# Two layers of a hybrid encoder on one core: part of the feed-forward down projections by seven products

## The reference, cut to what matters

```
def rmsnorm(x, g):
    xf = xf * lax.rsqrt(jnp.mean(xf * xf, axis=-1, keepdims=True) + EPS)
    return (xf * g).astype(x.dtype)

def swiglu(h, w_gate, w_up, w_down):              # 1024 -> 2816 -> 1024
    return (jax.nn.silu(h @ w_gate) * (h @ w_up)) @ w_down

x += 0.5*SwiGLU(RMSNorm x); x += Mixer(RMSNorm x); x += 0.5*SwiGLU(RMSNorm x)
```

## Time and profile before

| | |
|---|---|
| profiled execution, its own time | 1818.21 us |
| its span | 1816.3 us |
| TensorE busy | 1797.4 us (99%) |
| VectorE busy | 1331.8 us (73%) |
| ScalarE busy | 857.8 us (47%) |
| GpSimd busy | 51.7 us (3%) |
| DMA queue of SyncE | 174.49 MB, 31.4% of 16 engines |

### The profile page before, as it was taken

How to read it: one execution, slowest core, us unless ns; L and a number is a source line. 1 busy time by engine, 2 the same in 40 slices (tenths; PEclk the granted TensorE clock), 3 DMA queues, 4 the chain that set the end, 5 groups by cost and what they waited for, 6 DMA issues and landing times.

```text
span 1816.3 us, 32636 instructions
## 1 busy us (share of the span) xinstructions
PE 1797.4 (99%) x13408; PEld 1716.0 (94%) x13408; DVE 1331.8 (73%) x1826; ACT 857.8 (47%) x1403; POOL 51.7 (3%) x68
## 2 busy tenths in 40 slices
PE   9999999999999999999999999999999999999997
PEld 8999999999999999999999999999998899889986
DVE  7766887556768866887798578865646799578854
ACT  7443554335446543554565335543423565335542
POOL 0000000000000000000000000000123000000000
PEclk9999999999999999999999999999999999999999
DMA  5255233342222233223223332334222222332331
GB/s 179 84 96 117 94 117 102 108 126 69 60 81 81 94 100 102 97 99 110 89 93 101 102 101 93 108 103 123 84 70 70 70 84 103 109 101 94 111 113 56
DMA packets 81107, 176.87 MB, mean 97 GB/s; under 512 B 7292, under 2 KB 12700, under 8 KB 80960
## 3 DMA queue, kind: packets, MB, share of 16 engines
q1 hardware_dynamic: 80544, 174.49, 31.4%
q10 hardware_dynamic: 416, 0.29, 0.0%
HBM read 171.35 MB, written 3.41 MB: 96 GB/s over the span
## 4 chain that ended last, share of the span: by engine, by line
PE 94%; DVE 3%; ACT 1%; DMA 1%; issue 1%; SPq 0%; DVEq 0%; ACTq 0%
PE psum L2036 25%; PE psum L2106 13%; PE psum L2108 13%; PE psum L2109 13%; PE psum L2046 7%; PE psum L2045 4%; PE psum L2049 4%; PE psum L2044 4%; PE psum L2048 3%; PE psum L2156 2%; PE psum L2155 2%; PE psum L2157 2%; PE psum L2165 2%; DMA rb_sb<-in_rel_bias 0%; DVE wl L1231 0%
## 5 line engine op out<-in xcount | busy, mean ns | idle before, releaser
L2106 PE MATMUL psum<-fh,wh 128*128 128x264 f32 (+1 forms) x1968 | 560.2, 285 | 2.5 <-ACT psum L732 2.2
L2109 PE MATMUL psum<-fh,wl 128*128 128x264 f32 (+1 forms) x1968 | 557.3, 283 | 0.0
L2108 PE MATMUL psum<-fl,wh 128*128 128x264 f32 (+1 forms) x1968 | 556.7, 283 | 0.0
L2106 PEld LDWEIGHTS psum<-fh,wh 128*128 128x128 f32 x1968 | 371.1, 189 | 4.0 <-issue 3.0
L2108 PEld LDWEIGHTS psum<-fl,wh 128*128 128x128 f32 x1968 | 371.0, 189 | 0.5
L2109 PEld LDWEIGHTS psum<-fh,wl 128*128 128x128 f32 x1968 | 369.8, 188 | 0.0
L592 ACT ACTIVATE wh<-raw 128x1024 fp32r<-128x1024 f32 (+2 forms) x194 | 169.2, 879 | 228.4 <-PE psum L2036 176.6
L2036 PE MATMUL psum<-xs,wh 128*128 128x264 f32 (+1 forms) x1504 | 267.2, 297 | 4.5 <-DVE xs L1346 3.0
L1231 DVE TENSOR_TENSOR wl<-raw,wh 128x1024 fp32r<-128x1024 f32 (+2 forms) x193 | 195.6, 1021 | 96.7 <-ACT wh L592 96.3
L2036 PEld LDWEIGHTS psum<-xs,wh 128*128 128x128 f32 x1504 | 213.7, 189 | 14.8 <-issue 4.7
L2046 PE MATMUL psum<-hs,wh 128*128 128x512 f32 x528 | 206.6, 391 | 0.0
(11 more groups left out here) (313 smaller groups left out, 2966.1 us busy)
## 6 DMA issues: line engine op xcount, KB each, us to landing
raw<-in_w_gate_up SPq DMA_DIRECT2D x175, 512.0 KB, 3.7
raw<-in_w_down SPq DMA_DIRECT2D x64, 384.0 KB, 3.2
raw<-in_w_down SPq DMA_DIRECT2D x64, 320.0 KB, 3.0
raw<-in_od_in SPq DMA_DIRECT2D x21, 512.0 KB, 3.5
raw<-in_ev_in SPq DMA_DIRECT2D x18, 512.0 KB, 3.5
raw<-in_ev_out SPq DMA_DIRECT2D x8, 512.0 KB, 3.5
raw<-in_od_out SPq DMA_DIRECT2D x8, 512.0 KB, 3.5
x<-in_x_t SPq DMA_DIRECT2D x8, 264.0 KB, 5.2
```

The costliest lines, as they stand in the source:

```text
L2106: pe.matmul(psum[:, bank, 0:w], wh[:, slot, cols], high_x, start=start and j == 0, stop=False, skip_group_check=True)
L2108: pe.matmul(psum[:, bank, 0:w], wh[:, slot, cols], low_x, start=False, stop=False, skip_group_check=True)
L2109: last = pe.matmul(psum[:, bank, 0:w], wl[:, slot, cols], high_x, start=False, stop=j == 3, skip_group_check=True)
```

## The change

Every feed-forward is now worked off in three passes of 6, 6 and 10 hidden tiles. The down projection of the first two passes is made by seven products as well, in two "down" groups a pass; each group gives output tiles 2d, 2d+1, 2d+4, 2d+5 (d = 0, 1) from six hidden tiles, so that a product has 3 tiles x 3 matmuls. In feed-forward 0 the first pass is made of the six standard tiles, with a standard down projection of six tiles; so seven passes in all have down groups. The third pass (10 tiles) is as before.

- The hidden tiles of these passes are paired as (j, j+3) and written as the seven activation forms (`hf`, folded on VectorE and ScalarE: `fold_first`, `fold_a_lows`, `fold_others`, `fold_b_lows`, `fold_a_highs`, `fold_b_highs`). The reciprocal root and the factor 0.5 are multiplied into them (`gate_a_root`, `gate_b_root`, scalar 0.5), so the result is added to x directly (`upper_rows`, `lower_rows`).
- S3 and S1 are no longer added on VectorE. SyncE loads the first term (S3 has a fifth slot of `raw`), and GpSimd issues a transfer that adds the second term in place. All seven quarters are therefore loads.
- S4 is summed in place, the low part of A22 is written over its raw form. `wh` has seven slots, `wl` five.
- Only one group in a feed-forward has the entering form; the first of two down groups ("turn") leads too. TensorE's products in a turn are split: first the two known tiles of three, the last one later.
- The plain P2 stays in the first two groups of feed-forwards 1 to 3 alone.
- The bias table is stored by pairs of rows behind the loads of four groups of the last pass of feed-forward 0.
- Scratch tensors of the mixers move; the first loads of feed-forwards 1 and 3 wait for the first output tile of the mixer.
- All orders are written out for eleven kinds of groups.

```diff
-PASS_F0 = (0, 10)
-PASS_F = (10, 12)
+PASS_F0 = (0, 6, 12)
+PASS_F = (6, 6, 10)
+TURNED = 2
...
+            JOBS += [(_q, _p, "up", _j) for _j in range(PASS_F[_p] // 2)]
+            if _p < TURNED:
+                JOBS += [(_q, _p, "down", _d) for _d in range(2)]
...
+def plain(g):
+    q = JOBS[g][0]
+    return q > 0 and not is_down(g) and g < ENTERED[q] + 2
...
+            def steady_group(g):
+                quarter_load("a12", g)
+                if not ends(g):
+                    quarter_load("s3", g + 1)
+                    quarter_load("s1", g + 1)
+                quarter_load("a22", g)
+                if not ends(g):
+                    quarter_load("a11", g + 1)
...
+                    if q == 0 and not folds(g) and not is_down(g) and not ends(g):
+                        table_rows(2 * (g - GROUP[q, 2][0]), 2 * (g - GROUP[q, 2][0]) + 2)
...
+            def accumulate_s3(g):
+                slot = raw_slot("s3", g)
+                pool.wait_ge(raw_in[slot], RAW_COUNT["s3", g])
+                pool.dma_start(landing("s3", g), weights_of(JOBS[g][0], g, 1, 0), accum_op=ALU.add).then_inc(s3_added, 16)
+            def accumulate_s1(g):
+                slot = raw_slot("s1", g)
+                pool.wait_ge(raw_in[slot], RAW_COUNT["s1", g])
+                pool.dma_start(landing("s1", g), weights_of(JOBS[g][0], g, 1, 1), accum_op=ALU.add).then_inc(s1_added, 16)
...
+            def sum_s2(g):
+                dve.wait_ge(s1_added, 16 * (g + 1))
+                dve.wait_ge(a11_low, g + 1)
+                dve.tensor_tensor(raw_quarter("a11", g), raw_quarter("a11", g), raw_quarter("s1", g), ALU.add).then_inc(s2_sum, 1)
...
+            def folding_group(g, q, real):        # VectorE
+                n = 2 * g
+                c22(n - 1, real)
+                gate_a_root(g - 1, real)
+                sum_s4(g)
+                up_a_out(g - 1, real)
+                low_s1(g)
+                fold_first(g - 1, real)
+                gate_b_root(g - 1, real)
+                c21(n - 1, real)
+                low_s4(g)
+                up_b_gate(g - 1, real)
+                fold_a_lows(g - 1, real)
+                fold_others(g - 1, real)
+                low_a12(g)
+                fold_b_lows(g - 1, real)
+                c22(n, real)
+                low_a22(g)
+                low_a11(g + 1)
+                low_s3(g + 1)
+                sum_s2(g + 1)
+                gate_a_out(g, real)
+                c21(n, real)
+                low_s2(g + 1)
+                gate_b_scale(g, real)
...
+            def turn_group(g, q, real):           # VectorE
+                n = 2 * g
+                c22(n - 1, real)
+                gate_a_root(g - 1, real)
+                gate_b_root(g - 1, real)
+                sum_s4(g)
+                low_s1(g)
+                c21(n - 1, real)
+                up_a_out(g - 1, real)
+                low_s4(g)
+                fold_first(g - 1, real)
+                up_b_gate(g - 1, real)
+                fold_a_lows(g - 1, real)
+                fold_others(g - 1, real)
+                low_a12(g)
+                fold_b_lows(g - 1, real)
+                low_a11(g + 1)
+                low_a22(g)
+                low_s3(g + 1)
+                sum_s2(g + 1)
+                c22(n, real)
+                c22(n + 1, real)
+                c21(n, real)
+                low_s1(g + 1)
+                upper_rows(n, real)
+                c21(n + 1, real)
+                low_s2(g + 1)
...
+            def turn_group(g, q, real):           # TensorE
+                n = 2 * g
+                known, rest = range(reach(g) - 1), (reach(g) - 1,)
+                p4(n - 1, real)
+                p7(n, real, js=known)
+                p3(n - 1, real)
+                p1(n, real, js=known)
+                p1(n + 1, real, js=known)
+                p5(n, real, js=known)
+                p5(n + 1, real, js=known)
+                p1(n, real, js=rest)
+                p7(n + 1, real, js=known)
+                p1(n + 1, real, js=rest)
+                p6(n, real, js=known)
+                p2(n, real, js=known)
+                p6(n + 1, real, js=known)
+                p7(n, real, js=rest)
+                p7(n + 1, real, js=rest)
+                p2(n + 1, real, js=known)
+                p5(n, real, js=rest)
+                p5(n + 1, real, js=rest)
+                p6(n, real, js=rest)
+                p6(n + 1, real, js=rest)
+                p2(n, real, js=rest)
+                p4(n, real)
+                p2(n + 1, real, js=rest)
+                p3(n, real)
+                p4(n + 1, real)
+                p3(n + 1, real)
...
+            def folding_group(g, q, real):        # TensorE
+                n = 2 * g
+                p1(n, real)
+                p7(n, real)
+                p3(n - 1, real)
+                p4(n - 1, real)
+                p6(n, real)
+                p1(n + 1, real)
+                p5(n, real)
+                p6(n + 1, real)
+                p7(n + 1, real)
+                p2(n, real)
+                p2(n + 1, real)
+                p3(n, real)
+                p4(n, real)
+                p5(n + 1, real)
```

More of the change, by code:

```diff
@@ new lines, in form, with reach @@
+def form(g):
+    q, p, kind, _ = JOBS[g]
+    if enters(g):
+        return "entry" if q else "first_entry"
+    if leads(g):
+        return "turn"
+    if enters(g - 1):
+        return "after_entry" if q else "after_first_entry"
+    if leads(g - 1):
+        return "after_turn"
+    if ends(g):
+        return "last"
+    if is_down(g - 1):
+        return "up_after_down" if folds(g) else "straight_after_down"
+    return "folding" if folds(g) else "straight"
+def reach(g):
+    return PASS_F[JOBS[g][1]] // 2 if is_down(g) else 4
@@ new lines, in ups_before, with downs_before, turned_before, lows_before @@
+def ups_before(g):
+    return sum(not is_down(h) for h in range(g))
+def downs_before(g):
+    return sum(is_down(h) for h in range(g))
+def turned_before(g):
+    return sum(folds(h) and not is_down(h) for h in range(g))
+def lows_before(g):
+    return STD_F + 2 * sum(not folds(h) for h in range(g))
+def ring_place(g, i):
+    return (CHUNK[ENTRY[JOBS[g][0]]] + i) % RING
+def raw_slot(kind, g):
+    return 4 if kind == "s3" else ring_place(g, RAW_RING.index(kind))
+def high_slot(kind, g):
+    return HIGH_SPARE.index(kind) if kind in HIGH_SPARE else 3 + ring_place(g, HIGH_RING.index(kind))
@@ L91, in chunk_cols, with low_slot, ring_high @@
+def low_slot(kind, g):
+    return 4 if kind == "a11" else ring_place(g, LOW_RING.index(kind))
+def ring_high(n):
+    return 3 + n % RING
 def chunk_cols(n):
     for q in range(4):
-        for p in range(2):
-            if CHUNK[down_name(q, p)] <= n < CHUNK[down_name(q, p)] + COUNT[down_name(q, p)]:
+        for p in range(3):
+            name = down_name(q, p)
+            if name in CHUNK and CHUNK[name] <= n < CHUNK[name] + COUNT[name]:
                 return PASS_F[p] // 2 * P
@@ L2032, in passes @@
                 at = k if at is None else at
-                steps = ((wh, 0), (wh, 1)) if beside else ((wh, 0), (wh, 1), (wl, 0))
+                high, low = wh[:, 3 + slot, w], wl[:, slot, w]
+                steps = ((high, 0), (high, 1)) if beside else ((high, 0), (high, 1), (low, 0))
                 for p, (weights, part) in enumerate(steps):
                     for dst, tok in outs:
-                        last = pe.matmul(dst, weights[:, slot, w], both[:, at, part, tok],
+                        last = pe.matmul(dst, weights, both[:, at, part, tok],
                                          start=start and p == 0, stop=stop and p == len(steps) - 1)
@@ L2065, in from_x @@
                         between()
-                    if wide:
-                        last = ffn_passes(acc_slot(tile), n % RING, k, both, k, k == 0, k == KT - 1)
-                    else:
-                        last = passes(outs, n % RING, k, both, k, k == 0, k == KT - 1, beside)
+                    parts_of, at = both(k)
+                    last = passes(outs, n % RING, k, parts_of, k, k == 0, k == KT - 1, beside, at)
                 last.then_inc(chunk_done, 1)
```

1629 lines of the change are left out of this document (1091 added, 538 removed).

## The result

The changed kernel takes 1853.85 us (median of 4 runs, 1852.59 to 1856.25) against 1818.51 for the kernel before: ratio 1.0196, 95% interval 1.0184 to 1.0208. The forecast was 1807.2 with a range of 1790 to 1832. It was wrong: slower by 2% where faster by 0.6% was forecast.

What follows compares the result with a forecast made beforehand. The prediction took TensorE's own stream, fed without a gap, as the bound: 1818.2 - 25.8 - 1.4 - 2.2 = 1788.8, plus 15.4 (turns), 1.5 (rows), 0.5 and 1.0, gives 1807.2 us, range 1790 to 1832.

Steps and rivals of the forecast that it cites:

- TensorE's work removed: Seven six-tile down passes by seven products save 25.8 us, dropped plain float32 products 1.4, waits on a copy 2.2.
- The turn: From up to down products TensorE waits on VectorE's fold: 2.2 us per turn, 15.4 for seven, range 0 to 5 each.
- Folding groups without a wait: In folding groups VectorE's 19.3 us fit beside TensorE's 20.1 in the written order; no wait priced.
- The start of the first one: First feed-forward's start with a six-tile down pass: last two hidden parts arrive as TensorE reaches them; 0.5 us.
- Table rows: Two rows beside each of four groups: 1.5 us in all; from above 12 us in each of the first one or two.
- a loop of 12.4 + A: Steady group's cycle through S1 low, landing, adding transfer and S2 sum, against 20.1 us; A may be 7.8 us.
- late-addition rival: The adding transfer is late: every us of A over 7.8 paid in some 30 groups, 1873 at A = 10; chance 0.18.
- The adding transfer: GpSimd's transfer that adds S1's second term takes A = 5.2 us, between 3.7 and 8.7; priced at nothing.
- Its sign at A = 8.2: Adding transfer's latency A at which the late-addition rival turns the change from faster to slower: 8.2 us.
- Free turns: Rival: the turn from up to down products costs nothing; 1789 to 1795, say 1791; chance 0.16.
- dear turns: Rival: turns cost 4 to 5 us each, so the seven passes win nothing; 1825; chance 0.14.
- the sign named in the prediction for its own failure: Wrong if TensorE waits once per steady group, with VectorE's S2 sum waiting for the DMA, or if turns have no wait.

Runs made afterwards that it cites:

- e4: e1's kernel with the second transfers of S3 and S1 plain, these sums left out of the computation: 1805.32 us, 0.9928 of before.
- e6: e4's kernel without VectorE's two products with the root in the folding groups: 1803.76 us.
- e1: The changed kernel with its eight table rows stored earlier, in the first straight stage and first down projection: 1820.1 us, ratio to before 1.0013.
- e5: The changed kernel, table rows in their place, with the second transfers of S3 and S1 plain, without the addition: 1834.08 us.
- e7: e1's kernel with three moves in VectorE's order (first S3 low earlier, up product before S4 sum, gate product before S2 sum): 1816.31 us, ratio 0.9992.
- e9: e1's kernel with e7's moves except the gate product's, and P4 of the last down output ahead of the new group's P7: 1815.13 us, ratio 0.9975.

## Why the prediction was wrong, step by step

- **TensorE's work removed, 25.8 + 1.4 + 2.2: nearly held.** With the rows moved and the addition out, the kernel stands at 1805.3. The forecast without its 1.5 for the rows is 1805.7, and that it comes so close is partly luck. By feed-forward, e4 against before: -0.9, -4.4, -4.4 and -3.7 us. In the second and third, where 2 x 3.86 = 7.7 was forecast, the gaps grew by 2.2, so 4.4 + 2.2 = 6.6 us of matmuls are gone. The window counts of the earlier trace rows take in matmuls that only reach into the window (167 counted, 164 start there): from start to start one of 264 columns takes 0.122 us, not 0.1198, and one of the five-matmul step 0.144, not 0.1418. That leaves 3.7 us a pass; the rest of the difference isn't explained. The lower cost of the turns made up for it.
- **The turn, 2.2 us each: right in kind, too high.** Three gaps of 0.85, 0.41 and 0.48 between starts, 1.37 us above the spacing in all, at five turns and 1.5 at the last two: 9.9 us against 15.4. VectorE's timeline agrees with the chain as said. Its roots hardly matter (e6); the piece behind the up product is what is left.
- **Folding groups without a wait: held** in e4 for the later feed-forwards. The start of the first one, priced at 0.5, has gaps of 0.96, 0.31 and 1.02 there: 1.9 us above the spacing.
- **Table rows, 1.5 us, at most 12: the step that failed, 33.8 us.** The price of a row was nearly right: some 4 us of all engines, where its packets fill 4.3 to 4.5. What was wrong is what the rows were weighed against: the engines' time (21 of 20.1 us) and VectorE's slack, while the step above them had given the adding transfer 7.8 us in a loop of 12.4 + A. The engines never were the limit (DMA share 0.53 to 0.86 in the five windows), but the adding transfer stood behind the rows for 9 to 11 us. With A = 16.1 and 16.4 as measured that loop is 28.5 and 28.8 us; the gaps follow each other by 29.3, 27.3 and 28.1. The formula of the late-addition rival was right, its A was taken for a quiet queue, and nothing was asked of A under the rows. The bound of 12 us was no bound: "in each of the first one or two" assumed that a delay is made good, but every group got a new pair.
- **The adding transfer, A = 5.2 priced at nothing: failed too, 14.8 us.** In e1, among the 512 KB ones, its shortest is 5.65, its median 5.9 (S3) and 7.4 (S1), its longest 10.6. The budget of 7.8 is that of a steady group, and there it holds: the straight stages of the later feed-forwards have one wait in e1, of 0.9. At the entry of a feed-forward and behind down products there is less. These places had been priced for VectorE's work only. The Trainium skill, in "DMA: Bandwidth & Descriptors" (section "Anatomy of one DMA"), gives an estimated 3.2 us for a plain 512 KB from GpSimd; e4's plain ones of that size have 3.8 at the least and 4.0 in S3's median, and for the addition, which the page doesn't price, only e1 against e4 shows a figure.
- **The rivals.** Late addition (0.18) is what happened, in place: four groups by the rows and some 15 entries and ends by the addition, not 30 steady groups. Its sign at A = 8.2 can't be read off, since no run had one A. Free turns and dear turns both fell.
- **What would show it.** TensorE waits once per group, and VectorE's S2 sum waits for a transfer, 33.6 us in four times (L1663 above): the sign named in the prediction for its own failure was the one that came, in the four groups with rows.

The account: 1805.3 (work, turns, plain transfers) + 14.8 (addition) + 33.8 (rows) = 1853.9. It adds up by its making, since the last two are differences of measured medians. The interaction of the last two is 5 us by e5's medians, not clear of their intervals, and 7 us by the straight stages. Not settled: what of the 14.8 is the later landing and what the 1.5 us of engines that each addition takes, and why the runs of kernels with additions differ by up to 12.5 us among themselves (e1; 10.7 in e7, 6.8 in e9, 3.7 in the changed kernel), those without by 0.6 to 3.1. No run tells these apart.

## What to carry to other kernels

Where a transfer is one link of a loop that closes once per group, its price is its landing under everything that is in flight at that place, and a budget in a steady group doesn't cover entries and ends. Take the cost of a small transfer from a stretch where it is alone: bytes say nothing when 26 GB/s keep the engines 80% busy. And ask for the time during which others stand still behind it (here 5.7 to 6.0 us a row), not only for the engine time that it fills (4.3 to 4.5). A long transfer that nobody waits for belongs where nothing on the chain loads; here the first straight stage and the first down projection took all eight rows for nothing.

## What the hardware showed that was not expected

- Two rows of 160 KB, each read from one partition and sent 128 times, take 11.4 to 12.0 us from first to last packet and fill 8.6 to 8.9 us of the 16 engines, at 26 GB/s; weight loads move about 400 GB/s. The first packet of a transfer issued beside them by GpSimd came 9.4 to 11.0 us after its issue, against 1.9 otherwise.
- The addition doubles the packets of these transfers, adds 1.9 to 2.2 us to the median landing of 512 KB, 1.5 us of all engines, and takes GpSimd 1.20 us to issue instead of 0.72.
- Which queue issues the rows (SyncE's or ScalarE's) changed nothing in the time, 1853.85 and 1853.31 us, though it changed when the first packets of the transfers beside them start.
- Behind a wait of 5 to 9.5 us the granted clock is at its lower level for 2.8 to 5.2 us; in the 20 us windows it reads 0.74 to 0.95, and it cost 7.5 us on top of 28.9.
